# Forgetting attention with two heads in step, its denominators summed on GpSimd, and P V in batches

## What is computed

```python
def _fox_prompt(q, k, v, logf):
    ...
    c = jnp.cumsum(logf, axis=1)
    ...
        s = jnp.einsum('bqhd,bkhd->bhqk', qi, k, preferred_element_type=jnp.float32) * scale
        s = s + ci[..., :, None] - c_k[..., None, :]
        ...
        s = jnp.where(kpos[None, :] <= qpos[:, None], s, NEG_INF)
        p = jax.nn.softmax(s, axis=-1)
        return jnp.einsum('bhqk,bkhd->bqhd', p, v.astype(jnp.float32))
```

## Time and profile before

| | us |
|---|---|
| median of 3 runs | 3879.26 (3877.65 to 3888.87) |
| profiled execution | 3885.66 |
| its span, first to last instruction | 3884.2 |
| the changed stage in it | 689.5 to 1205.5 |
| TensorE busy over the span | 3600.0 (93%) |
| VectorE, ScalarE, GpSimd busy | 1490.8 (38%), 1034.0 (27%), 698.6 (18%) |

### The profile page before, as it was taken

One profiled execution on the slowest core, in us unless ns is written; L12 is line 12 of the kernel. 1 busy time (PEld: TensorE's weight loads), 2 busy tenths in 40 slices (PEclk: granted clock), 3 DMA queues, 4 the chain that ended last, 5 costly groups with the idle time before them and its releaser, 6 DMA issues. The chain is left out here.

```text
span 3884.2 us, 48487 instructions
## 1 busy us (share of the span) xinstructions
PE 3600.0 (93%) x17963; PEld 2806.4 (72%) x18008; DVE 1490.8 (38%) x3105; ACT 1034.0 (27%) x1500; POOL 698.6 (18%) x672
## 2 busy tenths in 40 slices
PE   7999998699995999978997889999997899999999
PEld 7987787355552777764443778888886788888888
DVE  2223333354552555524332233434343333333333
ACT  3322222244441333332222321121112311111111
POOL 2223466330000011110232200000000210000000
PEclk9999999799997899989998999999998899999999
DMA  5546766664645565357886021111104111111111
GB/s 197 195 162 208 227 206 195 170 178 134 179 135 153 146 175 146 124 213 298 322 296 206 34 76 44 49 59 43 43 33 168 36 55 44 43 43 43 43 43 60
DMA packets 295926, 507.42 MB, mean 131 GB/s; under 512 B 79153, under 2 KB 204594, under 8 KB 283186
## 3 DMA queue, kind: packets, MB, share of 16 engines
q1 hardware_dynamic: 271538, 378.14, 32.0%
q10 hardware_dynamic: 6136, 71.65, 5.1%
q0 software_dynamic: 18080, 55.33, 4.0%
HBM read 408.18 MB, written 164.50 MB: 147 GB/s over the span
## 5 line engine op out<-in xcount | busy, mean ns | idle before, releaser
L2467 DVE TENSOR_TENSOR fin_x<-mlp_y,fin_x 128x512 f32<-128x512 f32 x544 | 350.0, 685 | 751.7 <-PE mlp_y L2510 751.7
L2487 PE MATMUL mlp_u<-fin_h_hi,mlp_w_hi 128*128 128x512 f32 (+2 forms) x1280 | 451.9, 353 | 29.0 <-DVE mlp_w_lo L2443 29.0
L2489 PE MATMUL mlp_u<-fin_h_hi,mlp_w_lo 128*128 128x512 f32 (+2 forms) x1280 | 451.6, 353 | 0.0
L2488 PE MATMUL mlp_u<-fin_h_lo,mlp_w_hi 128*128 128x512 f32 (+2 forms) x1280 | 451.4, 353 | 0.0
L2508 PE MATMUL mlp_y<-mlp_w_hi,mlp_u_hi 128*128 128x512 f32 x1088 | 423.8, 389 | 1.3 <-DVE fin_x L2467 1.3
L2509 PE MATMUL mlp_y<-mlp_w_lo,mlp_u_hi 128*128 128x512 f32 x1088 | 424.3, 390 | 0.0
L2510 PE MATMUL mlp_y<-mlp_w_hi,mlp_u_lo 128*128 128x512 f32 x1088 | 423.9, 390 | 0.0
L2427 POOL TENSOR_TENSOR mlp_u<-mlp_r 128x1024 f32<-128x1024 f32 (+2 forms) x80 | 131.7, 1646 | 1330.2 <-ACT mlp_r L2368 1330.2
L666 PE MATMUL proj_z<-proj_w_hi,proj_x_hi 128*128 128x512 f32 (+1 forms) x816 | 310.0, 380 | 27.2 <-DMA proj_x_lo<-scratch_xt 13.0
L668 PE MATMUL proj_z<-proj_w_hi,proj_x_lo 128*128 128x512 f32 (+1 forms) x816 | 304.3, 373 | 0.0
L667 PE MATMUL proj_z<-proj_w_lo,proj_x_hi 128*128 128x512 f32 (+1 forms) x816 | 303.8, 372 | 0.0
(11 more groups left out here) (237 smaller groups left out, 6057.2 us busy)
## 6 DMA issues: line engine op xcount, KB each, us to landing
samp_k_in<-in_cache_k SPq DMA_DIRECT2D x128, 256.0 KB, 4.7
samp_v_in<-in_cache_v POOLq DMA_DIRECT2D x128, 256.0 KB, 4.7
mlp_w_raw<-in_w_up SPq DMA_DIRECT2D x64, 512.0 KB, 4.6
mlp_w_raw<-in_w_down SPq DMA_DIRECT2D x64, 512.0 KB, 4.2
out_new_win_k<-in_win_k ACTq DMA_DIRECT2D x8, 4080.0 KB
out_new_win_v<-in_win_v ACTq DMA_DIRECT2D x8, 4080.0 KB
proj_x_hi<-scratch_xt SPq DMA_DIRECT2D x34, 512.0 KB, 6.4
proj_x_lo<-scratch_xt SPq DMA_DIRECT2D x34, 512.0 KB, 6.3
```

The lines of the kernel that those rows point to most:

```text
L2467: dve.tensor_tensor(part, y_ps[(tiles * par + t) % 2][0:rows, q * D_G:(q + 1) * D_G], part, ALU.add).then_inc(y_added, 1)
L2487: pe.matmul(out, hi, h_hi[:, k, c0:c0 + n], start=(k == 0), stop=False)
L2488: pe.matmul(out, hi, h_lo[:, k, c0:c0 + n], start=False, stop=False)
L2489: mm = pe.matmul(out, lo, h_hi[:, k, c0:c0 + n], start=False, stop=(k == KC - 1))
```

## The change

Heads go in four pairs, both heads of a pair in step. A unit is two key tiles for both heads, so four score tiles; a pair has 20 units. Three banks s_ps, sixteen places pT (four units). P V is no longer made behind each step: at every second unit TensorE makes the products of the two units before, eight in a row, the two heads into the two halves of the partitions of one bank o_ps, with 64 columns of V and no ones. The denominators come from GpSimd: it adds up the exponentials of a macro in acc, and one pair of products with ones a macro puts the sums over partitions on all 64 rows of each head in x_ps. VectorE takes the reciprocal of 128x512, multiplies o_ps by it into o_f, TensorE turns that back (four of 128x128), ScalarE copies it out and stores it from its own queue. One bank x_ps serves all three, turns of maxima, denominators and turns back (take_x waits for the last reader). The split of the maxima is gone from VectorE: kb's two last rows now select a head and the turned row holds both heads' maxima. Loads come in pieces of 512 columns from SP's queue, which now also moves the pages, four between loads. The number and size of scores, exponentials and low pieces is as before.

```diff
-    spread(range(FOX_BASE[2], FOX_BASE[3]), 0, 7, 0)
...
+HEAD_PAIRS = HEADS // 2
+FOX_UNITS = [(m, 2 * k) for m in range(MACROS) for k in range(MACRO // 2 * (m + 1))]
+LOW_ORDER = [(m, x, j, z) for m in range(MACROS) for x in range(m + 1) for j in range(MACRO) for z in range(2)]
...
+        return 20 if kt < MACRO * m else 17 if kt == MACRO * m else 8
...
+            spans, turns = [None, (0, 1), (2, 5), (6, 10)], [None, 1, 5, 11]
...
+            spans, turns = [(-9, -8), (-7, -5), (-4, 2), (3, 9)], [-6, -3, 4, 11]
...
-    AHEAD = 2
-    PT_N = 4
+    S_BANKS = 3
+    PT_N = 16
...
+            for p in range(HEAD_PAIRS - 1):
+                for x in range(2):
+                    if p > 0:
+                        scores_done(p - 1, 17 + 2 * x)
+                    load_ka(p + 1, x)
+                    move_pages(4)
+                for m in range(2):
+                    scores_done(p, FOX_FIRST[m + 1] - 1)
+                    load_q(p + 1, m)
+                    move_pages(4)
+                for x in range(MACROS):
+                    sp.wait_ge(maxed, N_LOW * p + LOW_BASE[3] + 2 * MACRO * (x + 1))
+                    load_decay(p + 1, x)
+                    move_pages(4)
...
         @block.gpsimd
...
+            for G in range(UNITS):
...
+                        pool.wait_ge(exped, 4 * G + 2 * k + z + 1)
+                        if kt == 0:
+                            op = pool.tensor_tensor(to[:, x:Q_COLS], tiles[0][z][:, x:Q_COLS], tiles[1][z][:, x:Q_COLS],
+                                                    ALU.add)
+                        else:
+                            pool.wait_ge(acc_step, before[z])
+                            op = pool.tensor_tensor(to[:, x:Q_COLS], to[:, x:Q_COLS], tiles[k][z][:, x:Q_COLS], ALU.add)
+                        op.then_inc(acc_step, 1)
...
+                pool.wait_ge(acc_step, steps)
+                pool.sem_inc(added, 1)
...
         @block.scalar
...
+            def fetch_back(n):
+                act.wait_ge(o_turned, n + 1)
...
+                act.activation(o_sb[:, n % 2, :, :], x_ps[:, :].rearrange("p (j d) -> p j d", d=P), ACT.Copy)\
+                    .then_inc(returned, 1)
...
+                    if G >= 4:
+                        act.wait_ge(pv, G - 3)
+                        act.wait_ge(added, G - 3)
...
+                for n in ended(G - 3):
+                    fetch_back(n)
...
         @block.vector
...
+            def take_off(p, m):
+                dve.wait_ge(m_turned, turn_order.index((p, m)) + 1)
...
+                dve.tensor_copy(qb[HD:HD + 2, :, m, :], x_ps[0:2, :].unsqueeze(1).to_broadcast([2, 2, Q_COLS]))\
+                    .then_inc(m_set, 1)
+
+            def post(n):
+                dve.wait_ge(den_done, n + 1)
...
+                dve.reciprocal(rden[:, :], x_ps[:, :]).then_inc(inverted, 1)
+                dve.wait_ge(inverted, n + 1)
...
+                dve.tensor_tensor(o_f[:, n % 2, :], o_ps[n % 2][:, :], rden[:, :], ALU.mult).then_inc(posted, 1)
...
+            for G in range(UNITS + 2):
+                for todo in planned(G, "low"):
                     largest(*todo)
+                for n in ended(G - 2):
+                    post(n)
+                for todo in planned(G, "turn"):
                     take_off(*todo)
...
         @block.tensor
...
-                pe.matmul(o_ps[n % 2][0:HD + 1, x:Q_COLS], v_in[:, h % 2, kt, :], pT[:, g % PT_N, x:Q_COLS],
-                          start=(kt == 0), stop=(kt == MACRO * (m + 1) - 1)).then_inc(pv.sem, 1)
...
+                for k in range(2):
+                    x = reach(kt + k, m)
+                    for z in range(2):
+                        mm = pe.matmul(o_ps[n % 2][half(z), x:Q_COLS], v_in[:, z, kt + k, :],
+                                       pT[:, (4 * G + 2 * k + z) % PT_N, x:Q_COLS], start=(kt + k == 0),
+                                       stop=(kt + k == MACRO * (m + 1) - 1))
+                mm.then_inc(pv, 1)
+
+            def denominators(n):
+                take_x()
+                pe.wait_ge(added, last_unit(n) + 1)
+                for z in range(2):
+                    mm = pe.matmul(x_ps[half(z), :], c["ones"][:, 0:HD], acc[:, n % 2, z, :], start=True, stop=True)
+                mm.then_inc(den_done, 1)
...
+            for G in range(UNITS + 3):
+                todo = planned(G, "low")
+                for k in range(4):
+                    if G < UNITS:
+                        scores(G, k // 2, k % 2)
+                    for x in todo[len(todo) * k // 4:len(todo) * (k + 1) // 4]:
+                        low_scores(*x)
+                if G % 2 == 1:
+                    for x in (G - 2, G - 1):
+                        if 0 <= x < UNITS:
+                            values(x)
+                for n in ended(G - 2):
+                    denominators(n)
+                for x in planned(G, "turn"):
+                    turn_max(*x)
+                for n in ended(G - 3):
+                    turn_back(n)
```

More of the change, by code:

```diff
@@ L1032, in turn_back, with half @@
-            def turn_back(h, m):
-                n = MACROS * h + m
-                o_out.wait(pe, h, m)
-                posted.wait(pe, h, m - 1)
-                for j in range(MACRO):
-                    mm = pe.transpose(back_ps[:, j, 0:HD + 1], oT[:, n % 2, j * P:(j + 1) * P],
-                                      c["ident"][0:HD + 1, 0:HD + 1])
-                mm.then_inc(o_turned.sem, 1)
+            x_count = iter(range(len(uses)))
+            def half(z):
+                return slice(z * HD, (z + 1) * HD)
@@ new lines, in take_x, with low_scores @@
+            def take_x():
+                k = next(x_count)
+                if k > 0:
+                    kind, count = uses[k - 1]
+                    pe.wait_ge(inverted if kind == "den" else m_set if kind == "turn" else returned, count)
+            def low_scores(p, o):
+                m, x, j, z = LOW_ORDER[o]
+                n = min(Q_COLS, (MACRO * m + j + 1) * P - x * Q_COLS)
+                pe.wait_ge(q_loaded[m], 48 * (p + 1))
+                ka_arrived(pe, p, x)
+                if N_LOW * p + o >= 2:
+                    pe.wait_ge(maxed, N_LOW * p + o - 1)
+                mm = pe.matmul(low_ps[o % 2][:, 0:n], qa[:, z, m, j * P:(j + 1) * P], ka[:, z, ka_slot(p, x), 0:n],
+                               start=True, stop=x < m)
+                if x == m:
+                    mm = pe.matmul(low_ps[o % 2][:, n - P:n], ident_bf[:, :], mask_bf[:, P:2 * P], start=False, stop=True)
+                mm.then_inc(scored_low, 1)
```

487 lines of the change are left out of this document (262 added, 225 removed).

## The result

The changed kernel took a median of **3934.5 us** (3929.2 to 3947.1, four runs) against 3878.5 (3875.0 to 3888.9, four runs) of the kernel before in the same comparison: ratio **1.0145**, 95% interval 1.0113 to 1.0176. It is slower, by 56 us or 1.45%; the forecast was 3885 and its range ended at 3920. The profiled execution of the changed kernel has a span of 3935.6 us, 51.4 over the 3884.2 of the profile before.

The account below looks back on a forecast made before the run. TensorE, and P V in it, was taken to bound the stage. A pair's 119.6 us, less 27.7, plus 2.6, 12.4, 4.5, 1.5 and 8.0, gave 120.9; four pairs and +1 for ends made +6: 3885 us, range 3840 to 3920.

Parts of the forecast that it names:

- case A: Whole stage: the clock falls behind each stall, a pair takes 120.9 us against 119.6, total 3885 us; chance 0.45.
- rival C: The clock stays down longer or falls also after short waits: +10.8 us a pair, about 3928 us; chance 0.12.
- TensorE's demand: TensorE's own work for a pair of heads falls from 119.6 to 94.5 us.
- P V in halves: P V products of two heads run side by side in one bank's halves: -27.7 us a pair.
- Rival E: P V: the halves take turns instead of running side by side, +27.7 us a pair, about 3996 us; chance 0.02.
- VectorE's reciprocal: Denominators: the reciprocal, now of 128x512 instead of 128x4, takes 3.34 us, 16 times.
- The stall behind each post: TensorE idles 3.1 us while VectorE does reciprocal and product ahead of the next maxima, four a pair: +12.4 us.
- Rival B: The stalls come out a little shorter than 3.1 us and the clock holds: -26 us, 3853 us; chance 0.35.
- The single bank: x_ps serves turns, denominators and turns back, so TensorE waits for VectorE's copy: 3 x 1.5 us, +4.5 a pair.
- The clock, the term that decides: Behind each of a pair's four stalls, 4.6 us at half clock, 2.0 us of it lost: +8.0 us a pair.
- Ends: Stage's start and tail: first score 14 us earlier, 9 given back by early low pieces, tail +6: together +1 us.
- D: GpSimd's adds of exponentials become the bound, shut out by VectorE, 145 us a pair: 3980 us; chance 0.06.

Follow-up runs that it names:

- e12: e6 with P V behind every unit in batches of four instead of behind every second unit in batches of eight: 3861.2 us, ratio 0.9943.
- e6: e5 with each turn of the maxima moved from the end of its unit to its middle, from the second pair on: 3857.8 us, ratio 0.9937.
- e11: e6 with each P V batch ordered head by head, four products into one half of the bank, then four into the other: 3909.8 us, ratio 1.0069.
- e9: Changed kernel with the reciprocal of only the first 256 columns, the other 256 copied (division left out there): 3918.7 us, ratio 1.0087.
- e14: e6 with GpSimd's adds behind the first of a macro cut to 128 columns and the division left out: 3852.7 us, ratio 0.9913.
- e5: Changed kernel with denominators as 128x8, division after the turn back, and the last macro's query load moved from SP's to ScalarE's queue: 3880.1 us, ratio 0.9993.
- e13: e6 with a macro's first values loads issued behind the next macro's queries, keys and decay: 3861.9 us, ratio 0.9947.

## Why the prediction was wrong

The forecast's case A had the right chain and got its sum wrong; of the times forecast, that of the rival C, 3928 us, lies nearest to the 3934.5 measured. Per term, in the interval from first to last score (what was forecast for a pair, times 4):

| term | forecast | measured |
|---|---|---|
| TensorE's work at full clock | -94 | -75 |
| TensorE idle | +68, and +9 in the first two units | +73 |
| low clock | +32 | +49 |
| sum | +15 | +47.7 |

How the measured sum falls to the first and the third row rests on the 0.39. e12, with 11 us of low clock, says the same: 426.1 - 0.39 x 11, less 15 for its small sums (32.7 against 17.3) and some 10 for its shorter batches, is 397 us at full clock, and the changed kernel's is 398.

**Three steps of the forecast failed, by 17 to 19 us each: the clock behind the stalls, TensorE's demand, and the start of the stage.**

- **P V in halves** (-27.7 a pair). The mechanism is right and so is the price: 3.65 us for eight products (3.59 to the next start in e6), 3.6 forecast; e11 shows that the halves do run side by side. Rival E falls.
- **VectorE's reciprocal** (3.34 us). It took 3.358. The straight line through three short rows held; the 4.3 us worked out from the repeat count in the Trainium skill (VectorE: DVE Perf Modes, First, the fixed hardware budget) are not what this chip took.
- **The stall behind each post** (3.1 us, 12.4 a pair). 2.75 on average over fourteen; right. Rival B, that the clock would hold if the stall were half a microsecond shorter, falls: two of the three stalls of 2.5 us had 3.4 us at half clock behind them, and e9, with stalls of up to 2.0, has 122 us of it.
- **The single bank** (3 waits of 1.5 us a pair, 18 in all). 8.3 and 9.6 us; right in size. e6 shows that they are on the path.
- **The clock, the term that decides** ("behind each I take 4.6 us at half clock ... +8.0"). This is **the first step that failed**. The mechanism is right, its size is not: 131 us were low, not 73.6, and at 0.39 that is 51 us (49 over the kernel before), not 32. Behind the fifteen posts in the interval it was 6.6 us each, not 4.6, or 2.6 us lost each, not 2.0: nine of the fourteen stalls had 6.8 us or more behind them, four 3.4, one none until a wait for a load. That is 7 us of the miss. The 18 us at the start of the interval, where low pieces are fed by VectorE and no stall stands, and the 14 us behind loads and a short wait make the other 11; the sum had nothing for either. That waits of 1.4 us leave the clock alone (1.6 us in the trace) held for five of the six waits of 1.35 us before a macro's first score; behind the sixth, to 954.46, it was low for 3.4 us. I had kept a longer fall for C with a chance of 0.12, from a sample of three; its 6.5 us behind each post came, its fall behind every short wait didn't, so that its 3928 us came so near is partly luck: the rest of the miss is in terms that C had as A had them.
- **TensorE's demand** (94.5 us a pair, and 1.5 for the low pieces fed by VectorE). This is **the second step that failed**. 449.1 - 0.39 x 131 = 398 us at full clock, against 473 before: 19 us less of a gain than summed, nearly 5 a pair. Taking each TensorE row of e12 from its start to the next one's, the excess is with the low pieces: they hold it for 87 us where 0.235 us for each 512 columns make 64, and their mask products for 16 where they held it for 7 before; the scores' products give back 8 of it (151 against 160). e14's profile shows that GpSimd is not behind it. The starts in e12 show where most of it goes. 111 of its 312 low pieces start 0.14 to 0.17 us behind the end of VectorE's work on an earlier one, 91 of them within 5 ns of each other (0.145 to 0.150); in the kernel before no 5 ns hold more than 16 of 308. They were waited for, in waits too short for the view, since a record's modelled end covers them: the low pieces and masks ahead of these hold TensorE some 12 us longer than is usual for them. Those ahead of a batch of P V hold it some 9 us longer. So most of the excess is waiting for VectorE and the going over to a batch, priced in my sum at 1.5 a pair and at the 0.16 inside a batch; these are sums of starts, no run takes either away. In the rows, the first mask holds TensorE for 0.04 us, the second for 0.25, since the low piece behind it had to wait for VectorE, done at 948.91, and the third for 0.16 ahead of the batch.

```profile
947.97 0.23 PE L1147 MATMUL fox_low<-fox_mask_bf,fox_ident_bf 128*128 128x128 bf16 x1
948.01 0.48 PE L1174 MATMUL fox_s<-fox_qa,fox_ka 128*128 128x512 f32 x1
...
948.81 0.23 PE L1147 MATMUL fox_low<-fox_mask_bf,fox_ident_bf 128*128 128x128 bf16 x1
948.83 0.08 DVE L1064 DVE_READ_ACCUMULATOR2_ANT fox_piece_max<- 128x1 f32 x1
949.06 0.47 PE L1144 MATMUL fox_low<-fox_ka,fox_qa 128*128 128x512 f32 x1
949.37 0.23 PE L1147 MATMUL fox_low<-fox_mask_bf,fox_ident_bf 128*128 128x128 bf16 x1
949.53 1.94 PE L1191 MATMUL fox_o<-fox_pT,fox_v_in 128*64 128x512 f32 x8
```

- **Loads within the stage** (SP's queue, at nothing). 7 us of waits: I had counted SP's issues, 66 us of 113, but not that a single issue can stand 10 us in the queue. e5 shows the price once the stalls no longer hide it, 16 us.
- **Ends** (start -14, tail +6). The first score came 3.3 us later than before, not 14 earlier: fewer bytes ahead of the first low piece didn't bring it forward (22.5 us of waiting instead of 24.3, and the stage itself began 5 us later in this profile). This is **the third step that failed**, by 17 us; what the first loads wait for stays open (e13). The tail, from last score to the first low piece of the next stage, is 42.3 us against 31.6: +10.7 where +6 was summed; the granted clock of its first 17 us is 0.71, and it waits 2.9 us for GpSimd.
- **GpSimd** (D, 85 us a pair, hidden). Its adds took 1276 ns, 1.30 forecast, and it waits for ScalarE. D, GpSimd as the bound at 3980 us, falls; a cost of a few microseconds is not excluded (e14).

The terms together miss 33 us in the interval, 17 at the start and 5 in the tail, 55; the stages behind were 10 us shorter in this profile than in that before, which no edit here explains.

That no change was forecast had one more reason: a gain of 23.6 us a pair stood against losses of 24.9, so a miss of a few microseconds in any term decided the sign, and three of them missed to the same side.

## What to carry to other kernels

When an engine that had been full gets a stall, price the clock with it: here fourteen stalls of 2.75 us on average and what stood beside them came with 131 us at half clock, and idle time and clock together took 30 us a pair where the products had saved 19. Before dividing, look at which way the denominators lie: 128x8 took 0.2 us where 128x512 took 3.4, and a long operation on an engine that feeds another in strict order is paid by the other. And don't count a stall as the only obstacle: of those beside it one grew when it went (the waits for a late load, from 7 to 18 us) and one stayed (one bank for three uses), and they had to be removed one by one before the change paid.

## What was not expected of the hardware

- The granted clock stood low behind one of six waits of 1.35 us in the changed kernel. Behind the first pair, with no wait over 1.3 us, it was still low for 20 us with batches of eight (e6), and for 7 with batches of four (e12); the rest of their 39 and 11 us stands in the first 26 us of the interval.
- Four fp32 products into one half of a bank and then four into the other take 5.42 us, alternating 3.65. The former is 0.68 us a product, less than the 0.86 of the products of 65 rows before; the records in the middle of the batch, where the halves change, start twice as densely as those at its ends.
- A reciprocal of 128x128 took 0.95 us between other VectorE work and one of 128x512 3.36 us, so cutting it in four costs 0.4 us.
